# Masked attention of the second stack: row sums taken in the query-major score pass, their logarithm subtracted in the transposed pass, and no ones columns

## The reference, cut to what matters

```python
def _masked_softmax(logits, mask):
    s = jnp.where(mask, logits, NEG_INF_2)
    m = jnp.max(s, axis=-1, keepdims=True)
    e = jnp.where(mask, jnp.exp(s - m), 0.0)
    return e / jnp.maximum(jnp.sum(e, axis=-1, keepdims=True), TINY)

    p_w = _masked_softmax(s_w, m_w)                       # s_w: q.k * scale + rel_bias
    o_win = jnp.einsum('bhqk,bkd->bhqd', p_w.astype(vw.dtype), vw)
    return g[0] * o_cmp + g[1] * o_slc + g[2] * o_win     # NSA: three gated branches
    w = p[:, :, 0] - lam * p[:, :, 1]                     # differential: two softmaxes
    return jnp.einsum('bhqk,bhkd->bhqd', w.astype(v.dtype), v)
```

## Time and profile before

| | us |
|---|---|
| device time, median of three runs | 3042.01 |
| lowest and highest | 3035.91, 3046.28 |
| span of the profiled execution | 3024.6 |
| PE busy in it | 2838.6 (94%) |
| DVE, ACT, POOL busy | 1431.3, 1064.8, 244.5 |
| attention stage, layer 0 and layer 1 | 153.0, 157.7 |

### The profile page before, as it was taken

The page is one execution under the profiler, slowest core; times in us unless marked ns, Lnnn a source line. Parts: engine busy times, 40 slices in busy tenths (PEclk is TensorE's granted clock), DMA queues, the critical chain, the costliest instruction groups (busy, mean ns, idle before and its releaser), DMA issues. The chain is left out here.

```text
span 3024.6 us, 46035 instructions
## 1 busy us (share of the span) xinstructions
PE 2838.6 (94%) x18362; PEld 2429.6 (80%) x18362; DVE 1431.3 (47%) x2279; ACT 1064.8 (35%) x1478; POOL 244.5 (8%) x218
## 2 busy tenths in 40 slices
PE   7999899999999989999898889999989888999998
PEld 6986899998896889999787546888878754678886
DVE  3643577732673277771423653533333255443342
ACT  3244434322333444332323333423332333342232
POOL 1001200010101210001100022000010002200001
...
GB/s 123 97 28 29 121 96 83 88 96 66 89 84 1 57 127 89 83 90 96 117 98 84 29 1 56 94 93 94 96 101 98 84 28 1 44 85 95 96 97 111
DMA packets 44783, 237.98 MB, mean 79 GB/s; under 512 B 4894, under 2 KB 14750, under 8 KB 21360
## 3 DMA queue, kind: packets, MB, share of 16 engines
...
## 5 line engine op out<-in xcount | busy, mean ns | idle before, releaser
L161 PE MATMUL psum<-u_up_a_hi,w_a_hi 128*128 128x264 f32 x1408 | 378.7, 289 | 16.5 <-DVE u_up_a_lo L1883 15.4
L162 PE MATMUL psum<-u_up_a_lo,w_a_hi 128*128 128x264 f32 x1408 | 374.6, 286 | 0.0
L152 DVE TENSOR_TENSOR w_mlp_b_lo<-ring,w_mlp_b_hi 128x1024 fp32r<-128x1024 f32 x128 | 156.9, 1226 | 331.7 <-ACT w_mlp_b_hi L145 331.7
L152 DVE TENSOR_TENSOR w_a_lo<-ring,w_a_hi 128x1024 fp32r<-128x1024 f32 (+1 forms) x154 | 187.7, 1220 | 214.8 <-ACT w_a_hi L145 212.2
L164 PE MATMUL psum<-u_up_a_hi,w_a_lo 128*128 128x264 f32 x1408 | 287.0, 285 | 0.0
L161 PEld LDWEIGHTS psum<-u_up_a_hi,w_a_hi 128*128 128x128 f32 x1408 | 266.1, 189 | 23.2 <-issue 14.6
L145 ACT ACTIVATE w_a_hi<-ring 128x1024 fp32r<-128x1024 f32 (+1 forms) x154 | 161.5, 1050 | 299.3 <-PE psum L164 298.1
L162 PEld LDWEIGHTS psum<-u_up_a_lo,w_a_hi 128*128 128x128 f32 x1408 | 265.8, 189 | 0.5
L145 ACT ACTIVATE w_mlp_b_hi<-ring 128x1024 fp32r<-128x1024 f32 x128 | 135.8, 1061 | 302.0 <-PE psum L164 301.3
L164 PEld LDWEIGHTS psum<-u_up_a_hi,w_a_lo 128*128 128x128 f32 x1408 | 220.5, 190 | 0.0
L161 PE MATMUL psum<-u_up_b_hi,w_mlp_b_hi 128*128 128x512 f32 x512 | 201.4, 393 | 9.7 <-DVE u_up_b_lo L494 9.7
...
## 6 DMA issues: line engine op xcount, KB each, us to landing
...
```

What stands on the lines that cost most here:

```text
L152: nc.vector.tensor_tensor(W["lo"][:, buf, 0:n], W["tiles"][:, slot, at:at + n], W["hi"][:, buf, 0:n].bitcast(F32), ALU.subtract).then_inc( ...
L161: nc.tensor.matmul(out[c], a_hi, b_hi, start=start, stop=False)
L162: nc.tensor.matmul(out[c], a_hi, b_lo, start=False, stop=False)
```

## The change

Each unit now sums its exponentials in the query-major pass, and the transposed pass subtracts maximum plus logarithm of the sum, so that `prob` is normalised when it is made.

- ACT: after each `maxima`, `sum_exponents` runs one Exp for each head over the scores, in place in PSUM, with the maximum as a per-partition bias and a sum as accumulator output; after a unit's fourth, a small Ln (`log_of_sums`). Ln and Exp of bank 7 are gone.
- DVE: the custom instruction writes the biased scores back to PSUM; signs are turned so that it takes minima; the far minimum enters it as its start value, and the join is gone. `split_maxima` waits for `logged` and has three small instructions in place of two. `copy_mixed` multiplies with the gate, or adds the second differential half, itself.
- PE: `mix` has two matmuls per step, not four. Bank 7, now free, takes the scores of every second step (both heads share it, so their matmuls are issued apart, `score_first` and `score_second`) and the side jobs. The order of the steps is 512, 256, 384, 128 keys. A score waits for `summed`, not for `maxed`.
- POOL: only the additions onto the gated branch, and the low parts of `y`, are left; the memsets of the ones are gone.

The diff, cut to its core:

```diff
-    SIDES = (1, 2, 3, 7)
+    SIDE_BANK = 7
+    ORDER = (0, 2, 1, 3)
+    SIDES = (0, 1, 2, 3, 4, 7)
...
+    def score_out(n, pos, h):
+        w = P * (K - ORDER[pos])
+        if n == 0:
+            return ps[:, 2 * (pos % 2) + h, 0:w]
+        return ps[:, 7, NEAR * h:NEAR * h + w] if pos % 2 else ps[:, h, 0:w]
...
+                if n and pos % 2 == 0:
+                    pe.wait_ge(summed.sem, summed.at(layer, K * n - 1 if pos == 0 else K * n + 1))
+                if pos == 0 and "selected" in UNITS_B[n]:
+                    pe.wait_ge(side_act.sem, side_act.at(layer, 4))
...
+                    pe.wait_ge(summed.sem, summed.at(layer, K * n if pos == 1 else K * n + 2))
+                if pos == 1:
+                    side_read(n)
+                pass_waits(pe, S)
+                score_heads(n, pos, (0,)).then_inc(half_scored.sem, 1)
+            def score_second(n, pos):
+                pe.wait_ge(half_scored.sem, half_scored.at(layer, 2 * (n - 1) + (pos + 1) // 2))
+                pass_waits(pe, S)
+                score_heads(n, pos, (1,)).then_inc(scored.sem, 1)
...
-                for bank, at in ((6, (u["v"], u["v"] + 2 * DH)), (7, (u["v"] + DH, u["v"] + DH))):
-                    for h in range(2):
-                        mm = nc.tensor.matmul(ps[DH * h:DH * (h + 1), bank, c0:TB], v[:, j, at[h]:at[h] + DH],
-                                              prob[:, g % 2, h, 0:TB - c0],
-                                              start=(step == 0), stop=(step == K - 1), skip_group_check=True)
+                for h in range(2):
+                    mm = nc.tensor.matmul(ps[DH * h:DH * (h + 1), 6, c0:TB], v[:, j, u["v"] + DH * h:u["v"] + DH * (h + 1)],
+                                          prob[:, g % 2, h, 0:TB - c0],
+                                          start=(step == 0), stop=(step == K - 1), skip_group_check=True)
...
                 transposed(n, 0)
-                if n == U - 1:
-                    side(n, K * U)
+                if n == 1:
+                    side(0, K * n + 4)
+                if n in (7, 9):
+                    side(n, K * n + 4)
                 if following:
-                    score(n + 1, 1)
+                    if n in SIDES:
+                        score_first(n + 1, 1)
+                    else:
+                        score_second(n + 1, 1)
                 transposed(n, 1)
+                if following:
+                    if n in SIDES:
+                        score_second(n + 1, 1)
+                    score(n + 1, 2)
                 mix(n, 0)
-                if n == 1:
-                    side(0, K * (n + 1) + 2)
                 if following:
-                    score(n + 1, 2)
+                    score_first(n + 1, 3)
                 transposed(n, 2)
+                if following:
+                    score_second(n + 1, 3)
                 mix(n, 1)
-                if n in SIDES:
-                    side(n, K * (n + 1) + 3)
-                    transposed(n, 3)
-                    score(n + 1, 3)
-                else:
-                    if following:
-                        score(n + 1, 3)
-                    transposed(n, 3)
+                transposed(n, 3)
                 mix(n, 2)
                 if following:
                     turn_top(n + 1)
-                if n + 2 < U and "selected" not in UNITS_B[n + 2]:
+                if n in (1, 2, 3):
+                    side(n, K * (n + 1) + 4)
+                if n + 2 < U:
                     score(n + 2, 0)
                 mix(n, 3)
-                if n + 2 < U and "selected" in UNITS_B[n + 2]:
-                    score(n + 2, 0)
+                if n + 2 < U and n + 1 not in SIDES:
+                    score_first(n + 2, 1)
...
+            def sum_exponents(n, pos):
+                i = K - 1 - ORDER[pos]
+                act.wait_ge(maxed.sem, maxed.at(layer, K * n + pos + 1))
+                for h in range(2):
+                    out = score_out(n, pos, h)
+                    last = nc.scalar.activation(out, out, ACT.Exp, bias=neg_top[:, n % 2, h, i:i + 1], scale=-1.0,
+                                                accum_out=exp_sum[:, n % 2, h, i:i + 1])
+                last.then_inc(summed.sem, 1)
+            def log_of_sums(n):
+                act.wait_ge(summed.sem, summed.at(layer, K * (n + 1)))
+                nc.scalar.activation(log_sum[:, n % 2, :, :], exp_sum[:, n % 2, :, :], ACT.Ln).then_inc(logged.sem, 1)
...
+                exponent(n, 0)
+                if n == 0:
+                    act.wait_ge(side_dve.sem, side_dve.at(layer, D_C0 + 3))
+                    nc.scalar.activation(cn[:, :], cn[:, :], ACT.Exp).then_inc(side_act.sem, 1)
+                if n == 1:
+                    act.wait_ge(side_pe.sem, side_pe.at(layer, C_TURNED))
+                    nc.scalar.activation(pc[:, :], ps[:, SIDE_BANK, :], ACT.Copy).then_inc(side_act.sem, 1)
+                if n in (7, 9):
+                    norm_root((n - 7) // 2)
+                if following:
+                    sum_exponents(n + 1, 1)
+                exponent(n, 1)
+                if n in range(4, 8):
+                    early_high(n - 4)
+                if following:
+                    sum_exponents(n + 1, 2)
+                exponent(n, 2)
+                if n in (6, 8):
+                    norm_square((n - 6) // 2)
+                if following:
+                    sum_exponents(n + 1, 3)
+                    log_of_sums(n + 1)
+                exponent(n, 3)
+                if n == 8:
+                    early_high(4)
+                if following:
                     rows_of_maxima(n + 1)
-                    log_sums(n)
+                if n == 5:
+                    act.wait_ge(rows_out.sem, rows_out.at(layer, 7))
+                    nc.scalar.activation(sel_rows[:, :], top_rows[:, :].bitcast(F32), ACT.Copy).then_inc(side_act.sem, 1)
+                if n + 2 < U:
+                    sum_exponents(n + 2, 0)
...
-                    nc.vector.tensor_reduce(top[:, :, 2 + i], ps[:, bank:bank + 2, 0:far], AX_X, ALU.max)
+                    nc.vector.tensor_reduce(far_top[:, step, :], far_out(n, pos), AX_X,
+                                            ALU.min).then_inc(far_maxed.sem, 1)
+                    dve.wait_ge(far_maxed.sem, far_maxed.at(layer, 2 * n + step + 1))
                 for h in range(2):
+                    out = score_out(n, pos, h)[:, far:w]
                     last = nc.vector.tensor_tensor_reduce(
-                        junk[:, (K * n + step) % 2, h, 0:near], ps[:, bank + h, far:w],
-                        strips[:, u["strip"] + h, NEAR - near:NEAR], 1.0, -3e38, ALU.add, ALU.max, top[:, h, i:i + 1])
+                        out, out, strips[:, u["strip"] + h, NEAR - near:NEAR], 1.0,
+                        far_top[:, step, h:h + 1] if far else 3e38, ALU.add, ALU.min, neg_top[:, n % 2, h, i:i + 1])
                 last.then_inc(maxed.sem, 1)
-                if step == 1:
-                    dve.wait_ge(maxed.sem, maxed.at(layer, K * n + 2))
-                    nc.vector.tensor_tensor(top[:, :, 2:4], top[:, :, 2:4], top[:, :, 4:6], ALU.max).then_inc(joined.sem, 1)
             def split_maxima(n):
+                dve.wait_ge(logged.sem, logged.at(layer, n + 1))
                 dve.wait_ge(maxed.sem, maxed.at(layer, K * (n + 1)))
-                dve.wait_ge(joined.sem, joined.at(layer, n + 1))
                 if n:
                     dve.wait_ge(turned.sem, turned.at(layer, n))
                 else:
                     dve.wait_ge(cleared.sem, cleared.at(layer, 4 + 2))
-                by_tile = top[:, :, 0:4].rearrange("p h i -> p i h")
+                log, low_end = (x[:, n % 2, :, :].rearrange("p h i -> p i h") for x in (log_sum, neg_top))
                 first = HALF_ROW if UNITS_B[n].get("half") else 0
                 hi, lo = (top_turned[:, :, x:x + DH + 1:DH] for x in (first, first + 1))
-                nc.vector.tensor_copy(hi, by_tile).then_inc(split_top.sem, 1)
-                dve.wait_ge(split_top.sem, split_top.at(layer, 2 * n + 1))
-                nc.vector.tensor_tensor(lo, by_tile, hi.bitcast(F32), ALU.subtract).then_inc(split_top.sem, 1)
+                whole = shift[:, :, :].rearrange("p h i -> p i h")
+                nc.vector.tensor_tensor(hi, log, low_end, ALU.subtract).then_inc(split_top.sem, 1)
+                nc.vector.tensor_tensor(whole, log, low_end, ALU.subtract).then_inc(split_top.sem, 1)
+                dve.wait_ge(split_top.sem, split_top.at(layer, 3 * n + 2))
+                nc.vector.tensor_tensor(lo, whole, hi.bitcast(F32), ALU.subtract).then_inc(split_top.sem, 1)
...
                 dve.wait_ge(mixed.sem, mixed.at(layer, K * (n + 1)))
-                if u.get("onto") and n:
-                    dve.wait_ge(pooled.sem, pooled.at(layer, pool_steps(n)))
-                out = part_y[:, :] if u.get("onto") else y[:, u["y"], :]
-                if u.get("half"):
```

(9 more changed lines are left out.)

273 lines of the change are left out of this document (110 added, 163 removed).

## The result

The changed kernel takes 3079.2 us (median of 4, 3076.1 to 3080.2) where the kernel before takes 3039.0 beside it: a ratio of 1.0127, with a 95% interval of 1.0102 to 1.0152. It is slower by some 39 us. Forecast were 3027 us and a gain. The profiled execution has a span of 3074.3 us, 49.7 more than that of before. Its device time is 3076.1 us, 1.8 more than its span, and so it is in every run that has both; the 17 us given ahead of the prediction are wrong, and the trace of before, with 3024.6 us, shows one of the fastest executions of its kernel. 42 of the 49.7 us lie in the two attention stages. Most of the others lie ahead of the first one, which began 5.9 us later.

What follows compares the result with a forecast made beforehand. PE was taken to bound the kernel, a unit's middle by the chain PE, DVE, ACT, PE. Terms -9 + 4 + 2 - 4 - 8 gave -15 us, 3027 us from a median of 3042; range 3004 to 3050.

Steps and rivals of the forecast that it cites:

- Mixes: PE's mixes in each unit: half their matmuls go, 2.2 us a unit at full clock, 44 us over 20 units.
- ACT's sums: Row sums on ACT in each unit: 1.45 us for a pair of 512 keys, 4.5 us a unit.
- The loop: Chain DVE, ACT, PE through a unit at full clock: 11.5 us against 12.0, -9 us for 18 units.
- Prologue and tail: Stage start, with ACT's added sums: +2 us each, +4; stage end, with half the mixes: -2 each, -4.
- Side jobs: PE's queue waits behind `side_read` in units 2 to 4, unit 1 loses such a wait: +1 us a layer, +2.
- The clock: Units of both layers: six or seven drops to 1.2 GHz a layer, 1.7 us each, not 3.0: -8 us.
- slower by the clock: Rival: 1.2 GHz becomes the rule in the units, 15.0 us each, 270 against 260.2; 3056 us, chance 0.15.
- clock no worse: Rival: the units' loop as walked, clock term -26 us and sum -33; 3009 us, chance 0.13.
- The signs: Expected in the units: PE below 75%, its largest wait ACT's sums, some 1.4 us each; wrong if clock near 0.6.

## Why the prediction was wrong

**Mixes, right.** 320 matmuls in place of 640, and at 2.4 GHz the units get shorter where nothing else is late (11.96 us for 13.4 in unit 3 of the kernel without ones columns).

**ACT's sums, right.** Forecast 1.45 us for a pair of 512; in unit 1 the pair starts at 1721.19 and the next exponential at 1722.53, so 1.34.

**The loop, right to 0.4 us.** Walked to 11.5. Once the side jobs are out of the way it is 11.88 in unit 2 and 11.95 in unit 4, the latter with three zero-weight matmuls in it. It was 12.0 before, so the term of -0.5 a unit was -0.1 or a little more: of the 2.2 us that PE saves most becomes idle time. DVE's minima cost more than assumed (491 ns for 0.41 us).

**Prologue and tail, nearly right.** For the prologue +4 were forecast, and +2.5 and +1.2 measured; for the tail -4, and -1.2 and -1.4 measured.

**Side jobs, a term far too small.** Forecast was +1 us a layer: a new wait behind `side_read`, set off because "unit 1 loses such a wait". Unit 1 didn't lose it (2.7 us, where it was 1.9), and units 2, 3, 4 and 7 gained one each: PE stands behind side jobs for 8.6 and 8.8 us in the two layers, where it was 1.9 in each. At full clock the halved mixes make up for much of this: unit 1 takes 14.75 for 15.1, and unit 2 13.92 with added zero-weight matmuls, for 13.3 before and 13.5 forecast. Reading the results early brought 33 us of the 39 back. In the two traces the units are 29.5 us shorter for it, 16 of it the waits themselves, the rest by a higher clock.

**The clock, the step that failed.** The term was "six or seven [drops] instead of three or four a layer" at "1.7 us where it was 3.0", giving -8. The count was not far off: eight of nine units of layer 0 are at 0.77 or below, and in layer 1 all are at 0.89 or below. The price was wrong. It scaled a drop as it had looked before, half a unit long (0.77), because "full stretches bring the clock back". They did not: in units 5 to 7 PE was nearly full and the clock stayed at 0.50 for 55 us. Unit 6 costs 15.26 us against some 12 at full clock, 3.3 and not 1.7, and the units with extra matmuls more (unit 8: 14.35 at full clock, 17.9 at 0.71, 20.3 at 0.54).

An estimate of a layer's units at full clock, from rows at 1.00 or near it: about 11 + 14.75 + 13.9 + 14 + 13.4 + 2 x 12 + 15.2 + 14.35 = 121 us, with 13.4 for unit 4 as 12 and its side wait of 1.4. They took 149.6 and 151.4, so the clock costs some 60 us. Counted in the same way, with 118.5 a layer, it cost the kernel before 23 at most, as its units 7 and 8 have more mixes than the rows used for them. So the clock term was some +37 and not -8, and loop and side jobs together some +4 and not -7. These two, 45 and 11 us, turn the -15 into +41, and the stages grew by 42. All this rests on one execution each; in the traces of the kernel before with small edits the same units took 262 to 270 us, against 260 here, so each term can be 10 us off.

**How the two go together.** Halving the mixes alone costs nothing and gains nothing: the clock takes the gain back. The 39 us came with the rest of the change, and in the changed kernel another place for the side jobs gets 33 of them back.

**The rival "slower by the clock" was nearest to this case,** given 0.15 and 3056 us. Its 15.0 us for a unit were measured as 15.26. It took that for all 18 units; side jobs and extra matmuls at 1.2 GHz came on top, 301 us for 270. The argument set against it, the return of the clock, was read off units whose mixes still had the ones columns. The rival "clock no worse" has a clock term of -26 that no row gives: without drops it would be -34.

**The signs.** PE was to be busy for less than 75% of a unit, and was for 87%, as its work went at the lower clock. ACT's sums were to be PE's largest wait: they are 8.1 us, about 1.0 each, and the side jobs' 8.6 are more. "A clock near 0.6" was named as a sign of being wrong, and came.

The Trainium skill (TensorE: Matmul & The Clock Gate, What's actually happening) says that the clock follows how busy PE has been of late. By busy time alone these runs do not fit it: at 95% busy, unit 6 of the changed kernel stays at 1.2 GHz, while its unit 1, busy for 9.97 of 14.75 us, has 2.4.

**What stays open.** What brings the clock down, and what would keep it, was not isolated. The rows show what PE did: in units 5 and 6 its scores and transposed products use 32 of the 128 partitions, and only the mixes and the turn of the maxima use all. Halving the mixes (the kernel without the ones columns) or doubling them (each mix twice, with the side jobs early) moved the clock with them, 0.90 and 0.87 to 0.69 and 0.77, and 0.68 and 0.65 to 0.81 and 0.80. That partitions are the reason is not shown, and the changed order lowers the clock too, by what isn't known. Matmuls of all partitions with zero weights held it in units 1 to 3 and mostly not in units 5 and 6; as their weights are zero, they don't show what real ones would do. Why one execution of a kernel recovers in unit 7 and the next does not isn't shown either.
